# Two projections that load their first weight tile elsewhere, and a gated linear attention in one block with its gates, norm and output product

## The reference

```python
def _gla_mixer(h, w_in, gate_w2, gate_b, gla_norm, w_out):
    q, k, v, r, g_lr = _split(h @ w_in, L1_SPLITS)
    q = q.reshape(bsz, s, GLA_HEADS, GLA_HEAD_DK) * GLA_HEAD_DK ** -0.5
    ...
    logits = jnp.einsum('bsdr,drk->bsdk', g_lr, gate_w2) + gate_b
    la = (jax.nn.log_sigmoid(logits.astype(jnp.float32)) / GLA_TAU).reshape(bsz, s, 2, GLA_HEADS, GLA_HEAD_DK)
    o = _bidirectional(_gla_scan, (q, k, v, la[:, :, 0]), (q, k, v, la[:, :, 1]))
    o = _head_rmsnorm(o.reshape(bsz, s, GLA_DV), gla_norm, GLA_HEADS) * jax.nn.silu(r)
    return o @ w_out
```

## Time and profile before

| | |
|---|---|
| median of 3 runs | 2932.11 us (2931.83 to 2934.81) |
| the profiled execution | 2931.59 us, its span 2929.8 us |
| PE busy | 2686.9 us, 92% of the span |
| DVE, ACT busy | 1311.1 us (45%), 1177.7 us (40%) |
| mean granted clock of TensorE | 0.952 |

### The profile page before, as it was taken

One profiled execution on the slowest core, in us unless ns is written; L12 is line 12 of the kernel. 1 busy time (PEld: TensorE's weight loads), 2 busy tenths in 40 slices (PEclk: granted clock), 3 DMA queues, 4 the chain that ended last, 5 costly groups with the idle time before them and its releaser, 6 DMA issues. The chain is left out here.

```text
span 2929.8 us, 39491 instructions
## 1 busy us (share of the span) xinstructions
PE 2686.9 (92%) x16552; PEld 2287.7 (78%) x16552; DVE 1311.1 (45%) x1671; ACT 1177.7 (40%) x1616; POOL 42.0 (1%) x79
## 2 busy tenths in 40 slices
PE   5999998998999998999989989979887899777998
PEld 3677785876777785888768879979777899776998
DVE  3222235455322235222346554446545675444675
ACT  3222225444322225232245544443445564334653
POOL 3000000000000002000000000000000000000000
PEclk8999999999999999999999989989888999888999
DMA  8666422212566424223223235445301454321453
GB/s 277 212 204 214 151 73 86 58 58 85 188 207 205 165 77 110 86 86 114 86 72 87 79 123 172 161 142 174 118 1 62 146 194 153 121 90 58 148 169 115
DMA packets 277178, 375.50 MB, mean 128 GB/s; under 512 B 11020, under 2 KB 232696, under 8 KB 276912
## 3 DMA queue, kind: packets, MB, share of 16 engines
q1 hardware_dynamic: 228288, 300.56, 30.9%
q10 hardware_dynamic: 46576, 69.26, 7.1%
q0 software_dynamic: 2176, 3.67, 0.8%
HBM read 372.33 MB, written 1.16 MB: 127 GB/s over the span
## 5 line engine op out<-in xcount | busy, mean ns | idle before, releaser
L458 PE MATMUL ps<-uh,wh 128*128 128x256 f32 (+1 forms) x4160 | 1394.1, 335 | 57.1 <-DVE ul L828 30.9
L459 PE MATMUL ps<-ul,wh 128*128 128x256 f32 (+1 forms) x4160 | 1378.7, 331 | 0.0
L460 PE MATMUL ps<-uh,wl 128*128 128x256 f32 (+1 forms) x4160 | 1377.5, 331 | 0.0
L458 PEld LDWEIGHTS ps<-uh,wh 128*128 128x128 f32 x4160 | 798.0, 192 | 174.4 <-issue 76.4
L449 DVE TENSOR_TENSOR wl<-ring,wh 128x2048 fp32r<-128x2048 f32 x212 | 482.2, 2275 | 918.7 <-ACT wh L444 811.6
L460 PEld LDWEIGHTS ps<-uh,wl 128*128 128x128 f32 x4160 | 798.2, 192 | 72.9
L459 PEld LDWEIGHTS ps<-ul,wh 128*128 128x128 f32 x4160 | 798.7, 192 | 69.1 <-issue 0.7
L444 ACT ACTIVATE wh<-ring 128x2048 fp32r<-128x2048 f32 x156 | 298.5, 1914 | 724.7 <-PE ps L460 348.3
L1060 DVE TENSOR_TENSOR wl<-ring,wh 128x2048 fp32r<-128x2048 f32 x66 | 151.3, 2292 | 322.3 <-ACT uh L1078 284.4
L1057 ACT ACTIVATE wh<-ring 128x2048 fp32r<-128x2048 f32 x66 | 126.3, 1914 | 338.4 <-PE ps L460 319.0
L1479 ACT ACTIVATE wh<-ring 128x2048 fp32r<-128x2048 f32 (+2 forms) x38 | 70.0, 1842 | 124.6 <-PE ps L460 124.6
(11 more groups left out here) (316 smaller groups left out, 2036.8 us busy)
## 6 DMA issues: line engine op xcount, KB each, us to landing
ring<-in_ffn_wi_dram SPq DMA_DIRECT2D x88, 1024.0 KB, 7.5
arena<-in_w_ada_dram ACTq DMA_DIRECT2D x42, 1536.0 KB, 6.8
ring<-in_ffn_w_up_dram SPq DMA_DIRECT2D x44, 1024.0 KB, 7.4
ring<-in_ffn_wo_dram SPq DMA_DIRECT2D x20, 2048.0 KB, 7.9
ring<-in_ab_w_in_dram SPq DMA_DIRECT2D x13, 2048.0 KB, 7.8
ring<-in_ffn_w_down_dram SPq DMA_DIRECT2D x10, 2048.0 KB, 7.8
ring<-in_c_w_in_dram SPq DMA_DIRECT2D x6, 2048.0 KB, 7.9
ring<-in_w_in_dram SPq DMA_DIRECT2D x20, 512.0 KB, 6.0
```

The source lines that it names most:

```text
L458: pe.matmul(to, sh, mh, start=start and n == 0, stop=False)
L459: pe.matmul(to, sh, ml, start=False, stop=False)
L460: mm = pe.matmul(to, sl, mh, start=False, stop=stop and last)
```

## The change

- `ab_in` and `c_in` get `first=1`: tile 0 goes to slot 1, tile 1 to slot 0, and so on. `lead_high` and `listed` take the slot from the plan.
- In `c_in` the low-rank tile is second (granule 2), ahead of keys, values and `r`. The projection uses 4 banks (0 to 3) instead of 8. All of `gla_prepare` becomes steps between its granules (`GlaGates`), in banks 4 to 7: turns and gate products behind granules 3 and 4, softplus at 5 and 6, scans at 6 and 7, exponentials at 7 and 8, scaled keys at 8 and 9, their turns at 10 and 11, scaled queries at 10 and 11. Silu of `r` is made at the copy out (ACT's items) or behind it (DVE's items).
- `gla`, `head_norm` and the output product become one block, `gla_out`. Two granules of `c_out` are split ahead. ACT squares and copies each head's outputs; TensorE sums the squares of head hh - 1 ahead of the outputs of head hh; root, scaled outputs and high and low parts follow one head behind. The first granule's products begin with inputs 0 to 3, then the last head's sum, then inputs 4 to 7.

```diff
-        planned("ab_in", Weights(len(AB_SPANS), listed_tiles(a["ab_w_in_2"][0], AB_SPANS), count=granules(AB_SPANS)))
+        planned("ab_in", Weights(len(AB_SPANS), listed_tiles(a["ab_w_in_2"][0], AB_SPANS), count=granules(AB_SPANS), first=1))
...
-        C_SPANS = [[(512 * i, 512)] for i in range(6)] + [[(3072, 32)]]
-        planned("c_in", Weights(len(C_SPANS), listed_tiles(a["c_w_in_2"][0], C_SPANS), count=granules(C_SPANS)))
+        C_SPANS = [[(0, 512)], [(3072, 32)]] + [[(512 * i, 512)] for i in range(1, 6)]
+        planned("c_in", Weights(len(C_SPANS), listed_tiles(a["c_w_in_2"][0], C_SPANS), count=granules(C_SPANS), first=1))
...
-            split_high(act, key, 0, plan[key].slot(0), 0, raw, shaped, side(key, 0))
+            split_high(act, key, 0, 0, 0, raw, shaped, side(key, 0))
...
-        def listed(key, spans, items, norm, beside=None, silu_items=0):
+        def listed(key, spans, items, norm, beside=None, banks=8, silu=()):
...
-                            if n >= 8:
-                                pe.wait_ge(free.sem, free.at(n // 2 - 3))
+                            if n >= banks:
+                                pe.wait_ge(free.sem, free.at((n - banks) // 2 + 1))
...
                         last.then_inc(prod.sem, 1)
+                        between(g)
...
+            def tensor(self, pe):
+                at = self.LOW_GRANULE
+
+                def between(g):
+                    if g == at + 1:
+                        pe.wait_ge(act_free.sem, act_free.at(self.LOW_ITEM // 2 + 1))
...
+                    if g == at + 2:
+                        pe.wait_ge(low_weight_loaded.sem, low_weight_loaded.at(16))
+                        pe.wait_ge(low_copied.sem, low_copied.at(1))
...
+                    if g in (at + 8, at + 9):
+                        d = g - at - 8
+                        for half in range(2):
+                            pe.wait_ge(keys_ended.sem, keys_ended.at(2 * d + half + 1))
...
                 def _(pe):
...
+                    scores(0)
+                    for hh in range(GLA_HEADS):
+                        pe.wait_ge(states_made.sem, states_made.at(6 * hh + 6))
+                        if hh + 1 < GLA_HEADS:
+                            scores(hh + 1)
+                        if hh:
+                            sums(hh - 1)
+                        outputs(hh)
+                    pe.wait_ge(split.sem, split.at(1))
+                    first_products(range(EARLY), True, False)
+                    sums(GLA_HEADS - 1)
+                    first_products(range(EARLY, KD), False, True).then_inc(prod.sem, 1)
+                    w.tensor(pe, 1)
...
                 def _(act):
...
+                    act.preload_act_table_set(LN_EXP)
+                    for g in range(AHEAD):
+                        w.high(act, g)
+                    for hh in range(GLA_HEADS):
+                        keep(hh)
+                        if hh:
+                            root(hh - 1)
+                            high_of(hh - 1)
+                    root(GLA_HEADS - 1)
+                    high_of(GLA_HEADS - 1)
...
                 def _(dve):
...
+                    states(0)
+                    for hh in range(GLA_HEADS):
+                        if hh + 1 < GLA_HEADS:
+                            states(hh + 1)
+                        if hh == 0:
+                            for g in range(AHEAD):
+                                w.low(dve, g)
+                        if hh:
+                            made(hh - 1)
+                            low_of(hh - 1)
+                    made(GLA_HEADS - 1)
+                    low_of(GLA_HEADS - 1)
```

More of the change, by code:

```diff
@@ L1433, in _ @@
                     stream(sp, key)
+                @block.gpsimd
+                def _(pool):
+                    if beside is not None:
+                        beside.gpsimd(pool)
                 @block.tensor
                 def _(pe):
+                    between = beside.tensor(pe) if beside else lambda g: None
                     norm.tensor(pe)
@@ L1468, in take @@
                             else:
-                                eng.activation(to, of, ACT.Silu if n < silu_items else ACT.Copy, scale=scale).then_inc(free.sem, 1)
+                                eng.activation(to, of, ACT.Silu if n in silu else ACT.Copy, scale=scale).then_inc(free.sem, 1)
                 @block.scalar
@@ L2993, in two_blocks @@
         w2 = GM.take(2, 512)
-        GLA_SQ = GM.at
+        LA_AT = GM.at
         la = GM.take(2, GLA_HEADS, S)
@@ new lines, in then @@
+                        act.activation(qin[:, d], la[:, d], ACT.Exp, scale=1.0 / GLA_TAU).then_inc(decays_made.sem, 1)
+                    if g in (at + 9, at + 10):
+                        d = g - at - 9
+                        for half in range(2):
+                            n = 2 * d + half
+                            act.wait_ge(ends_turned.sem, ends_turned.at(n + 1))
+                            act.activation(ended[:, 2 * n:2 * n + 2, 1, :, :], ps[:, 4 + n, :].rearrange("p (k e c) -> p k e c", k=2, e=2), ACT.Copy)
@@ L3124, in gla @@
             C = GLA_CHUNK
+            w = Wide("c_out", flat_h, flat_l, KD, S, tail)
+            AHEAD, EARLY = 2, 4
             def chunk_sum(d, c):
@@ L3131, in gla, with _ @@
             with stage() as block:
+                @block.sync
+                def _(sp):
+                    stream(sp, w.key)
                 @block.tensor
@@ new lines, in first_products @@
+                    def first_products(ks, start, stop):
+                        _, shaped = w.granule(0)
+                        vh, vl = shaped(wh[side(w.key, 0)]), shaped(wl[side(w.key, 0)])
+                        for m in range(2):
+                            c = slice(m * P, (m + 1) * P)
+                            for kk in ks:
+                                if m == 0 and kk % 2 == 0:
+                                    pe.wait_ge(u_ready.sem, u_ready.at(kk // 2 + 1))
+                                last = multiply(pe, ps[:, m, 0:S], [((vh[:, kk, c], vl[:, kk, c]), (w.xh[:, kk, :], w.xl[:, kk, :]))],
+                                                start=(start and kk == ks[0]), stop=(stop and kk == ks[-1]))
+                        return last
@@ L3185, in _, with states @@
+                    w.tail_scalar(act)
                 @block.vector
                 def _(dve):
-                    for hh in range(GLA_HEADS):
+                    def states(hh):
                         gst = gst_two[hh % 2]
-                        dve.wait_ge(pe_step.sem, pe_step.at(2 * hh + 1))
+                        dve.wait_ge(chunks_scored.sem, chunks_scored.at(hh + 1))
                         for d in range(2):
@@ L3231, in two_blocks @@
                     lambda: ffn2(0, norm2(0, 2, mixer2_r[0]), (ffn2_r[0], "c_in")),
-                    lambda: c_project(norm2(1, 0, ffn2_r[0])), gla_prepare, gla,
-                    lambda: head_norm("c_out", GLA_SQ, (mixer2_r[1], ("up2", 1)), (0, KD, 2, "gla_norm", None, (ACT.Silu, gr))),
+                    lambda: c_project(norm2(1, 0, ffn2_r[0])), lambda: gla_out((mixer2_r[1], ("up2", 1))),
                     lambda: ffn2(1, norm2(1, 2, mixer2_r[1]), (ffn2_r[1], None)),
```

372 lines of the change are left out of this document (174 added, 198 removed).

## The result

| | before | after |
|---|---|---|
| median of the first runs | 2931.97 us (4 runs) | 2905.89 us (4 runs: 2905.71, 2906.06, 2906.52, 2895.76) |
| ratio | | 0.990 (95% interval 0.9884 to 0.9916) |
| the profiled execution | 2931.59, span 2929.8 | 2906.06, span 2904.3 |
| median of all runs in this document | | 2898.7 us (12 runs, 2893.27 to 2907.78) |

Faster by 26.1 us, 0.9%, clear of the interval. The first median is 13.6 us above the forecast of 2892.3 and 3.9 above its range; of the 39.8 us that were forecast two thirds came. Twelve runs of the same kernel, made in three lots, lie at 2893.3 to 2899.2 (seven) and 2905.3 to 2907.8 (five), so the 13.6 us have two parts: what the kernel really costs more than the walk (the sum of the prediction, step by step), and which of its executions were taken.

A forecast was written before the change was run, and what follows sets the result against it. TensorE, busy 8 or 9 tenths nearly everywhere, was taken as the bound, so time could come only from its rests. 2931.6 - 12.4 (lead-ins) - 28.9 (merged stages) + 2 (clock) = 2892.3 us, range 2883 to 2902.

The forecast's parts named there:

- Part 1: Lead-ins of `ab_in` and `c_in`: tile 0 issued early lands 5.4 and 7.0 us sooner, -12.4 us in all.
- Part 2: `gla_prepare` (25.7 us) hidden inside `c_in`: 6.0 us added on TensorE, 2.9 us for the change of block.
- rival (b): In `c_in` DVE becomes the bound, four to six splits come 1 us late: +5, 2897 us; chance 0.08.
- 68.6 + 6.0: Rest of `c_in`: its earlier length plus the transposes and gate products added on TensorE at full clock.
- 2 us for the clock: Allowance for TensorE's clock falling at the low-rank granule: a 3 us stretch at half and part of the gate products.
- the upper bound of 8: Clock's highest price: gate products at half 3.6, low-rank granule 2, two returns of 1.5 us.
- Part 3: `gla`, `head_norm` and `c_out` in one block: first granule of `c_out` ends 47.5 us into it.
- 44.6 + 2.2: Merged block's end: last 18 products start at 44.6 us, take 2.2 at full clock, 3.9 at half.
- After that nothing differs: Behind the first granule of `c_out` all stays as before, granules 1 to 3 following at 5.76 us.
- Rival (a): The clock's falls in `c_in` and the merged block take their full price: +6 more, 2898.5 us; chance 0.10.

The follow-up runs named there:

- e13: The kernel after, unchanged, one further execution with a profile: 2893.27 us.
- e7: The kernel after, with ACT's squares and DVE's additions ahead of the split of tile 0 before `ab_in` and `c_in`: 2899.14 us.
- e11: The kernel after with turned low-rank columns, root first, last head's sum behind 12 early products, tile 0 split between third and fourth square: 2890.53 us.
- e5: The kernel after, with the low-rank columns made already turned in products of 256 columns, without four transposes and a copy: 2898.64 us.
- e3: The kernel before, with the low-rank tile moved to second place in `c_in` and nothing merged: 2933.14 us, ratio 1.0004.
- e8: The kernel after with low-rank columns made turned, root ahead of the next head's square and copy, and squares ahead of tile 0's split: 2892.87 us.
- second lot: A later set of runs of the unchanged kernels before and after on the same chip: 2935.11 to 2895.88 us, 39.2 us less.
- e14: The kernel after, unchanged, another execution with a profile: 2898.17 us.
- e2: The kernel after without `first=1`, so both projections load tile 0 to slot 0 again: 2911.81 us.
- e4: The kernel after with 24 empty instructions ahead of SP's first load, nothing else changed: 2903.78 us.
- e6: The kernel after, with ACT's root and high part of the previous head ahead of the square and copy of the current one: 2901.5 us.
- e10: e6 with the sum over the last head's squares behind 12 of the 24 early products in TensorE's queue: 2892.23 us.

## Why the prediction was wrong

**Part 1, right.** Tile 0 had the early issue (0.4 us ahead of ACT's last split of the down product, as tile 1 had before), the loads landed after 8.9 and 8.2 us (8.2 and 7.9 assumed), and ACT's high part came 4.7 and 6.7 us earlier against them, in e13 5.4 and 6.9. The forecast was 5.4 and 7.0. The additions and the sum followed the tile, as said. What is late next is not just the tile, as e7 shows: squares, split and additions share ACT and DVE ahead of a block's end, and only with the split in their midst (e11) did TensorE's sum come another 1.5 and 0.7 us earlier, in front of `c_in` without a gain behind it.

**Part 2, right but for the clock.** TensorE has no gap in `c_in` (busy 79.16 of 79.20 us); rival (b) did not happen. DVE's latest low part, that of granule 10, ended 4.9 us into a granule of 5.76, where the walk had 5.0 to 5.3. The change of block took 2.4 us for 2.9. The rest of `c_in` was to take 68.6 + 6.0 = 74.6, with 2 us for the clock 76.6; it took 79.1 or 77.6. The step that failed is the size of that 2: the narrow granule's fall costs 1.4 to 2.9 us (granules 2 and 3 take 12.6 to 14.1 us, in e5 11.2), the gate products at half clock 1.5 or 3.0 more (11.1 or 12.6 us for 9.6). Without both it would be 79.1 - 2.9 - 1.5 = 74.7, so the 74.6 of the walk was right. The clock's full price in `c_in` is thus 4.4 us, or 2.9 in e13, where the forecast had 2; the upper bound of 8 had both at about their size. The cause was named rightly: narrow products (e3, e5).

**Part 3, right but for its end.** The period of the heads was 7.9 us (ACT's squares at 2630.42 and 2638.34), as walked; the chain behind the last outputs took 8.2 us in the walk and 8.3 in the trace (2644.8 to 2653.1). From the first score to the end of `c_out`'s first granule it was to be 47.5 us; it was 50.6, in e13 48.9. The last 18 products ran at half clock, 3.9 us and not 2.2, and these 1.7 us are more than the whole 1.4 of e13. Both prices stood in the prediction, and the lower was taken; its 44.6 + 2.2 is 46.8, and nothing in the walk says what the other 0.7 of its 47.5 is. The clock falls at these products in 12 of the 14 profiles of the merged block; in e7 and e8 it does not, with waits of the same size ahead of them, so the price is neither always paid nor set by the waits alone. The other 1.7 in after are the first head's scores and chunk sums at half clock (1.69 and 2.62 us, 1.13 and 1.57 in e13).

**"After that nothing differs", the step that failed most.** This sentence, and the sum from 2931.6 as a whole, took every stage that the change does not touch at its length in one profile. In the profile after, 1.9 us were lost ahead of `ab_in`, 5.1 between the two high parts, and 0.8 behind the block, all in code that is the same. With part 1's landings (1.0), `c_in` beyond its allowance (2.5) and the block and its change (3.1 - 0.6) that makes the 13.8 us between 2892.3 and 2906.06: 7.8 of them in stages that the change leaves alone, 6.0 at the places that it edits. In e13 the same account is +1.0: -1.8 up to ACT's high part of `c_in`, +1.0 in `c_in` beyond the allowance, -0.6 at the change of block, +1.4 in it, +0.9 behind it; the time was 2893.27.

So the mechanism and its place were right, and the price of the edit was right to a few us; the range was not. It came from the bounds of the edit alone, and the kernel's own executions differ by 14.5 us. Rival (a), 2898.5 (by its own sum 2898.3), is the nearest to the median of all twelve runs, 2898.7. That is in part luck: in e14, the profile nearest to that median, only 2.4 of the 6 us arose where (a) has them, 1.0 in `c_in` and 1.4 in the merged block. It is luck too that the second lot's 39.2 us meet the forecast's 39.8. Of the twelve runs, seven lie in the range.

The Trainium skill, TensorE: Matmul & The Clock Gate, "What's actually happening", has the clock set by how busy the engine was recently. By it the prediction had the merged stages at full clock and 2 us less; it set this aside because of the earlier trace rows, and the runs bear that out: the mean clock was 0.94 in `c_in` and 0.88 in the merged block, and behind the narrow granule PE was busy 8.30 of 8.30 us at 0.67. The page says in the same section that the number of slow products differs from run to run for the same kernel; six profiles of the kernel after agree, with 68 to 78 us at half clock in the mLSTM stages. It puts the price of the slow start at under 1% of a kernel and advises against fitting a count of slow products. Here the executions differ by 14.5 us, 0.5%, beside the 26 to 39 us that the change brought.

**Still open.** Whether the kernel after spreads wider than before at all: 37 runs of before lie at 2928.4 to 2937.5, but e3, which is before with one tile moved, has 12.6 us between its eleven. Whether part 1 makes the slow form of the mLSTM stages more frequent: the three profiles without `first=1` (before, e2, e3) have 386.6 to 388.5 us there, of the fifteen with it ten have 390.3 to 390.9 and five 387.5 to 388.2. And why the twelve fall in two groups: the executions of 2899.24 and 2898.17 each lack another fall, so the groups are not one fall each. A start moved by 24 empty instructions (e4) gave 2902.4 to 2904.8, between the groups, and does not settle it.

## What to carry to other kernels

Walk the queues of an edited block as here, but before trusting a sum to 5 us, read more than one execution and list where the clock falls in the stages that the edit leaves alone; that spread belongs in the range. Judge an edit of a few us by the length of its own stage between two fixed instructions, in more than one profile, and not by the median of four runs or its interval: by their medians e5 and e6 would have been read wrongly. When a step is moved to where its wait is hidden, check what stands ahead of it in every queue it depends on: e6 moved the right step on ACT and gained nothing until TensorE's queue followed (e10).

## What was not expected of the hardware

- Products of 32 columns let TensorE's clock fall even when it never rests: 48 of them, and the granule behind takes 7.1 to 8.5 us instead of 5.76 in 13 of 13 profiles; made as products of 256 columns, the same 32 weights cost no fall in 3 of 3. The wider form takes more columns and is 3.4 us faster.
- Gate products (16 rows of weights, 256 columns) run at full clock or lose it, for a longer or shorter time even in executions of the same kernel: with the granule around them they take 11.1 us in four profiles of after and 12.6 in two; in e4 and e11 they kept full clock, 9.6.
- The clock does not fall at once when TensorE has rested: in e10 four products behind a wait of 1.90 us ran at full clock, and then fourteen at half.
- The same kernel takes 2893.3 to 2907.8 us, with 236 to 280 us at half clock.
